# Down weights four rows to a partition, and the GLU product written in a new column order, in a two-layer decoder with a mixture of experts

## What is computed

```
def swiglu(h, w_gate, w_up, w_down):
    a = jnp.einsum('bsd,df->bsf', h, w_gate)
    b = jnp.einsum('bsd,df->bsf', h, w_up)
    return jnp.einsum('bsf,fd->bsd', jax.nn.silu(a) * b, w_down)
```

## Time and profile before

| | |
|---|---|
| median of three runs | 1541.46 us |
| span of the profiled execution | 1539.0 us |
| time of the profiled execution outside its span | not listed on its own; the median is 2.5 us above the span |
| TensorE (PE) busy | 1506.4 us, 98% |
| VectorE (DVE) busy | 1160.2 us, 75% |
| ScalarE (ACT) busy | 965.0 us, 63% |
| read from HBM | 432.10 MB |

### The profile page before, as it was taken

How to read it: one execution, slowest core, us unless ns; L and a number is a source line. 1 busy time by engine, 2 the same in 40 slices (tenths; PEclk the granted TensorE clock), 3 DMA queues, 4 the chain that set the end, 5 groups by cost and what they waited for, 6 DMA issues and landing times.

```text
span 1539.0 us, 20095 instructions
## 1 busy us (share of the span) xinstructions
PE 1506.4 (98%) x7122; PEld 1236.6 (80%) x7122; DVE 1160.2 (75%) x948; ACT 965.0 (63%) x854; POOL 11.0 (1%) x21
## 2 busy tenths in 40 slices
PE   7998999999999999999999999999999999999997
PEld 6877888887777888888888888888888888888885
DVE  4566554444546788898888888889889888888886
ACT  5554433444544677777677767777777777776775
POOL 0100000000000000000000000000000000000000
PEclk9999999999999999999999999999999999999999
DMA  9613655554540399999989989999999998998993
GB/s 356 244 56 125 204 182 189 191 191 164 167 161 16 123 345 367 331 346 366 367 320 370 358 314 374 360 337 349 366 336 343 370 367 314 370 366 319 359 373 114
DMA packets 184089, 433.61 MB, mean 282 GB/s; under 512 B 6963, under 2 KB 8011, under 8 KB 184060
## 3 DMA queue, kind: packets, MB, share of 16 engines
q1 hardware_dynamic: 182048, 426.80, 77.7%
q0 software_dynamic: 1776, 5.84, 1.1%
q10 hardware_dynamic: 236, 0.57, 0.1%
HBM read 432.10 MB, written 1.09 MB: 281 GB/s over the span
## 4 chain that ended last, share of the span: by engine, by line
PE 94%; DVE 3%; ACT 1%; issue 1%; DMA 0%; ACTq 0%; DVEq 0%; POOLq 0%
PE ps L1100 28%; PE ps L1102 28%; PE ps L1101 27%; PE ps L1263 2%; PE ps L1409 2%; PE ps L1191 2%; PE ps L1217 1%; DVE wlo L670 1%; PE ps L1203 1%; PE ps L1107 1%; DVE hn L688 1%; PE ps L1167 1%; PE ps L1433 0%; DMA gain<-in_mem_norm 0%; PE ps L1438 0%
## 5 line engine op out<-in xcount | busy, mean ns | idle before, releaser
L670 DVE TENSOR_TENSOR wlo<-raw,whi 128x2048 fp32r<-128x2048 f32 x404 | 921.8, 2289 | 246.2 <-ACT whi L414 244.7
L414 ACT ACTIVATE whi<-raw 128x2048 fp32r<-128x2048 f32 x404 | 772.1, 1914 | 257.8 <-PE ps L1102 255.6
L1100 PE MATMUL ps<-whi,xhi 128*128 128x512 f32 x1328 | 519.0, 391 | 6.2 <-DVE xlo L694 3.3
L1101 PE MATMUL ps<-wlo,xhi 128*128 128x512 f32 x1328 | 516.2, 389 | 0.0
L1102 PE MATMUL ps<-whi,xlo 128*128 128x512 f32 x1328 | 516.2, 389 | 0.0
L1100 PEld LDWEIGHTS ps<-whi,xhi 128*128 128x128 f32 x1328 | 249.3, 188 | 63.3 <-DVE wlo L670 7.0
L1102 PEld LDWEIGHTS ps<-whi,xlo 128*128 128x128 f32 x1328 | 249.2, 188 | 51.7
L1101 PEld LDWEIGHTS ps<-wlo,xhi 128*128 128x128 f32 x1328 | 249.3, 188 | 50.9
L1100 PE MATMUL ps<-whi,thi 128*128 128x512 f32 x560 | 226.8, 405 | 2.9 <-DVE tlo L828 2.9
L1102 PE MATMUL ps<-whi,tlo 128*128 128x512 f32 x560 | 221.5, 396 | 0.0
L1101 PE MATMUL ps<-wlo,thi 128*128 128x512 f32 x560 | 221.4, 395 | 0.0
(11 more groups left out here) (164 smaller groups left out, 685.5 us busy)
## 6 DMA issues: line engine op xcount, KB each, us to landing
raw<-in_moe_up SPq DMA_DIRECT2D x112, 1024.0 KB, 6.7
raw<-in_moe_gate SPq DMA_DIRECT2D x112, 1024.0 KB, 6.2
raw<-in_moe_down SPq DMA_DIRECT2D x112, 1024.0 KB, 6.6
raw<-in_ffn_up SPq DMA_DIRECT2D x14, 1024.0 KB, 5.1
raw<-in_ffn_gate SPq DMA_DIRECT2D x14, 1024.0 KB, 5.1
raw<-in_ffn_down SPq DMA_DIRECT2D x14, 1024.0 KB, 4.9
raw<-in_dil_w_in SPq DMA_DIRECT2D x10, 1024.0 KB, 5.0
raw<-in_swa_w_in SPq DMA_DIRECT2D x4, 1024.0 KB, 15.7
```

The costliest lines, as they stand in the source:

```text
L414: act.activation(whi[:, c % CUT, 0:span(c)], raw[:, c % RAW, 0:span(c)], ACT.Copy).then_inc(hi_ready, 1)
L670: dve.tensor_tensor(wlo[:, c % CUT, 0:n], raw[:, c % RAW, 0:n], whi[:, c % CUT, 0:n].bitcast(F32), ALU.subtract).then_inc(lo_ready, 1)
L1100: pe.matmul(dst, ahi, bhi, start=start, stop=False)
L1101: pe.matmul(dst, ahi, blo, start=False, stop=False)
```

## The change

Each partition now takes four neighbouring rows of the down weights in each step: partition p has the rows 4p, 4p + 1, 4p + 2 and 4p + 3 of the 512, the first two in the first unit and the last two in the second. The two rows of a unit lie side by side in HBM, 8 KB without a gap. The hidden columns have to be regrouped to match: block j must hold the columns 4p + j. `glu_mul` does that as it writes. It still reads the up product and SiLU in order, and writes column 4c + k of the 512 to place 128 k + c of `act_h`. Everything behind it is unchanged.

```diff
--- before.py
+++ after.py
@@ -143,9 +143,9 @@
     }
     chunk_w = {k: v.rearrange("z (k p) f -> p (z k) f", p=P) for k, v in chunk_w.items()}
     ffn_in = [w.rearrange("z (k p) f -> p (z k) f", p=P) for w in (ffn_up, ffn_gate)]
-    ffn_out = ffn_down.rearrange("z (k p) f -> p (z k) f", p=P)
+    ffn_out = ffn_down.rearrange("z (s p k) f -> p (z s) k f", p=P, k=FT)
     moe_in = [w.rearrange("z e (k p) f -> p (z e) k f", p=P) for w in (moe_up, moe_gate)]
-    moe_out = moe_down.rearrange("z e (k p) f -> p (z e) k f", p=P)
+    moe_out = moe_down.rearrange("z e (s p k) f -> p (z e s) k f", p=P, k=FT)
     gains = [mem_norm, norm_mix[0, :], norm_ffn[0, :], norm_mix[1, :], norm_ffn[1, :], final_norm]
 
 
@@ -326,9 +326,9 @@
                 for i in range(4):
                     load(FFN0 - 2 + i, s, ffn_in[i // 2][:, i % 2 * 4:i % 2 * 4 + 4, bass.ds(s * FCH, FCH)])
                 for i in range(2):
-                    load(FFN0 + 2 + i, s, ffn_out[:, bass.ds(s * FT - FT + 2 * i, 2), :])
+                    load(FFN0 + 2 + i, s, ffn_out[:, bass.ds(s - 1, 1), 2 * i:2 * i + 2, :])
             for i in range(2):
-                load(FFN0 + FFN_UNITS - 2 + i, 0, ffn_out[:, (STEPS - 1) * FT + 2 * i:(STEPS - 1) * FT + 2 * i + 2, :])
+                load(FFN0 + FFN_UNITS - 2 + i, 0, ffn_out[:, STEPS - 1:STEPS, 2 * i:2 * i + 2, :])
             load_chunks(C_DI, len(CHUNKS))
 
             def load_expert(job, e):
@@ -340,10 +340,10 @@
                              moe_in[i // 2][:, bass.ds(e, 1), i % 2 * 4:i % 2 * 4 + 4, bass.ds(s * FCH, FCH)])
                     for i in range(2):
                         load(MOE0 + 2 + i, job * STEPS + s,
-                             moe_out[:, bass.ds(e, 1), bass.ds(s * FT - FT + 2 * i, 2), :])
+                             moe_out[:, bass.ds(e * STEPS + s - 1, 1), 2 * i:2 * i + 2, :])
                 for i in range(2):
-                    f = (STEPS - 1) * FT + 2 * i
-                    load(MOE0 + FFN_UNITS - 2 + i, STEPS * job, moe_out[:, bass.ds(e, 1), f:f + 2, :])
+                    load(MOE0 + FFN_UNITS - 2 + i, STEPS * job,
+                         moe_out[:, bass.ds(e * STEPS + STEPS - 1, 1), 2 * i:2 * i + 2, :])
 
             with sp.Fori(0, NE) as job:
                 load_expert(job, job)
@@ -821,7 +821,8 @@
 
             def glu_mul(t, ev):
                 dve.wait_ge(silu_ready, ev + 1)
-                dve.tensor_tensor(act_h[:, t, :], ps[:, B_U[t], :], silu[:, t, :], ALU.mult).then_inc(act_ready, 1)
+                dve.tensor_tensor(free(act_h[:, t, 0:1], (1, P), (P, FT)), ps[:, B_U[t], :].rearrange("p (c k) -> p c k", k=FT),
+                                  silu[:, t, :].rearrange("p (c k) -> p c k", k=FT), ALU.mult).then_inc(act_ready, 1)
 
             def glu_tlo(t, ev):
                 dve.wait_ge(thi_ready, ev + 1)
```

## The result

The changed kernel takes 1547.45 us (median of 5 runs, 1547.22 to 1549.05) against 1541.99 us for the kernel before (5 runs): 1.0040 times as long, with a 95% interval of 1.0027 to 1.0053. It is slower by 5.5 us, or 6.3 us by the spans of the two profiled executions (1539.0 and 1545.3 us). The single runs of most kernels here fall into two groups some 1.5 us apart (the changed kernel: 1547.2 to 1547.5 and 1548.8 to 1549.1), so a median of five can stand in either.

A forecast was written before the change was run, and what follows sets the result against it. TensorE, busy for 98% of the span, bounds the kernel. Transfers 0, 48 expert loop steps 0, nine first steps (seven later experts', first expert's, dense part's) x 0.36 = 3.2 us: 1544.7 us, 0.2% slower; range 1540.6 to 1556.

The forecast's parts named there:

- the cover of 5.8 us for the loads: Expert loop: a down load lands 5.8 us before ScalarE reads its buffer, so a faster landing ends no wait.
- Edit 1: The down loads: 128 contiguous pieces of 8 KB in place of 256 of 4 KB; gain costed at zero.
- Edit 2: The GLU product L824 on VectorE: each result written 512 bytes past the last; 0.36 us more than 683 ns.
- two thirds of a slot: Extra time per hopping result in L824, a slot being 1.05 ns a column: 0.70 x 512 = 0.36 us.
- The pair it leaned on: Nearest VectorE writes with and without a hop, 175 and 174 ns: 0 to 2 ns a hop, 1 by its face.
- The cover of 0.37 us: Expert loop steps: L824 could end 0.37 us later before TensorE loses time at the transposes.
- a rival with a whole slot: L824 takes 0.54 us more, 0.17 us beyond the cover 48 times: 1554.5 us; chance 0.17.
- the band that had 0.42: The forecast itself: L824 takes 0.3 to 0.37 us more a product, 1544.2 to 1544.8 us; chance 0.42.
- The free write: L824's hopping write costs nothing, 1541.5 us; chance 0.24, with all up to 0.3 us a product.
- the worse loads: Down loads of long pieces take a tenth longer, stretching 56 expert steps by 0.56 us each: 1573 us; chance 0.04.
- the faster down matmuls: Long pieces bring the down product's matmuls from 395 to 389 ns, 10 us back: 1531 us; chance 0.06.
- A whole slot or more: L824 takes 0.54 us more (1554.5 us, chance 0.17), or 0.75 to 1.02 us more (1566 to 1582 us, chance 0.07).

## Why the prediction was right, point by point

- **What bounds the kernel.** Right. TensorE still fills its time but for the waits for the product, and the cover of 5.8 us for the loads was never touched. That a DMA share of 1.01 in a step is no bound is seen from two sides: in neither trace does a cut in the expert loops wait for a DMA, and a product that ends 0.05 us too late lengthens the step.
- **Edit 1, costed at zero.** Right: 1.0001, with the packets that were forecast.
- **Edit 2, the price of the write.** That the write costs something was right, the term was too small. I took two thirds of a slot, 0.36 us; measured were 0.35 to 0.38 us at the first steps and 0.42 in the loops, four fifths of a slot. The forecast's own limit, "wrong if L824 is above 1.06 us (then 57 waits instead of 9)", was passed: 57 waits. The trace of before could not show it, as it had no write with this pattern, and none beside a cut. That 0.36 us came as near as it did is in part luck. The pair it leaned on, L963 and L954, differs by one jump between two rows of eight neighbouring words, and the run with pairs shows that jumps between groups of neighbouring words are free: 256 of them left the product at 684 ns, where 1 ns each would be 0.26 us. So that pair says nothing of single words that hop, and the reason given for less than a whole slot, a port with free cycles, is shown by no run.
- **The Trainium skill's table** (Vector Engine (DVE) Microarchitecture Reference, "Measured stream behaviour on trn2"). Its 1.71 ns a column for a destination that hops 4 KiB at every element is close to this write where it is shortest, (1035 - 683)/512 + 1.05 = 1.74 ns; in the expert loops it is (1100 - 683)/512 + 1.05 = 1.86 ns. Its rule that pairs of adjacent words (starting on an 8-byte boundary, as these do) run at full rate agrees with the 684 ns of the pairs.
- **The cover of 0.37 us.** Right to a few hundredths: 0.42 us a product lost 0.06 a step, 0.44 lost up to 0.08, 0.07 lost none. That a late product ends 0.47 us before the next matmul is to be read in both timelines. One slip in counting has no effect: the dense layer has six loop steps with twelve products, not twelve steps.
- **The sum.** Forecast 3.2 us, of which the loops 0 and the first steps 3.2. Measured 5.5 us by the medians and 6.3 by the spans; of the latter some 3.3 are first steps, some 2.8 loops, and 0.2 lie outside of both. The term that was missed is 48 x max(0, 0.42 - 0.37), which the forecast had as a rival with a whole slot (0.54 us, 13 us). The truth lay between the two, 2.8 us above the forecast's time and 7 us below the rival's. By the forecast's own dividing line, 0.37 us a product, it falls on the side of that rival, which had a chance of 0.17; the band that had 0.42, 1544.2 to 1544.8, was missed. The result stayed in the range because the range reached past the rival. The margin between 0.36 us and 0.37 us of cover was too thin to count on: a write 0.06 us longer was enough to bring 48 steps into the sum.
- **The rivals.** The free write, the worse loads and the faster down matmuls (395 ns still) are all refuted: the first by L824's 1.09 us, the other two by the run with the loads alone. A whole slot or more is refuted as a size, since the write takes 0.42 us of a slot's 0.54.

## What to carry to other kernels

Where one engine is full, ask of each edge into it how late the producer may end; here that was 0.37 us, read by holding a place where the consumer waits against one where it doesn't, and it turned an instruction that got 0.41 us longer in 70 places into 5.5 us and not 29. Let neighbouring words stay in pairs when a VectorE write regroups columns; here single words that hopped cost 60% more for the whole instruction, and pairs nothing. A transfer that nobody waited for gave nothing back when it was made of longer pieces, though the DMA share of the step was 1.01.

## What the runs showed of the hardware that was not expected

- A hopping write does not have one duration. It took 1.03 to 1.06 us at the experts' first steps, 1.09 us in the dense loop with nothing on ScalarE beside it, and 1.10 to 1.11 us beside ScalarE's 128x2048 cut. Holding the cut back gave 1.07 to 1.08 us, so the cut is worth 0.02 to 0.03 us; the rest is open. The write in order stayed within 683 to 692 ns in all places.
- TensorE's load of a 128x128 float32 operand takes 140 ns from neighbouring columns and 205 to 210 ns from every second or every fourth one, the same for both steps.
- Transfers of 1 MB land nearly alike with pieces of 2, 4 and 8 KB: in the dense part 5.1, 4.9 and 5.1 us. The small step up from 4 to 8 KB is steady, though: down loads there landed after 4.8 or 4.9 us in the four traces with 4 KB pieces and after 5.0 or 5.1 us in the eight with 8 KB. In the expert loops, 6.0 to 6.7 and 6.4 to 6.9 us, the two overlap.
